# A head's Z-product records dealt unevenly over its 24 points, and one weight load moved ahead of a wait

## The reference

```python
h = rms_norm(x, g_norm[l]) * (1.0 + scale) + shift
proj = h @ w_in[l]
xa, va, oa, za, ia, fa, qa, ka, vat, zb, ga, gb = jnp.split(proj, split_at, axis=-1)
xc = jax.nn.silu(causal_depthwise_conv(xa, w_conv[l], b_conv[l]))
# q_m, k_m: xc times small matrices; 4 heads of width 256, chunked recurrence over the tokens
h_m = mlstm_chunkwise(q_m, k_m, v_m, ia + b_igate[l], fa + b_fgate[l])
h_m = rms_norm(sigmoid(oa) * h_m, g_mlstm_head[l]) + skip_mlstm[l] * xc
y_m = (h_m * jax.nn.silu(za)) @ w_out_mlstm[l]
# three attention groups (window, dilation) per head, merged by a softmax over their log-denominators
o_a = jnp.sum(wts[..., None] * jnp.stack(outs, axis=0), axis=0)
y_a = (o_a * jax.nn.silu(zb)) @ w_out_attn[l]
merged = jax.nn.sigmoid(ga) * y_m + jax.nn.sigmoid(gb) * y_a
x = x + gate * (merged @ w_out[l])
return rms_norm(x, g_final)
```

## Time and profile before

| | us |
|---|---|
| median of 3 runs (lowest, highest) | 1370.96 (1369.63, 1371.36) |
| the profiled execution: its own time | 1371.11 |
| its span in the profile | 1369.3 |
| PE busy | 1345.7 (98%) |
| DVE, ACT, POOL busy | 855.3, 580.1, 463.0 |
| chain that ended last: share of PE | 87% |

### The profile page before, as it was taken

One profiled execution on the slowest core, in us unless ns is written; L12 is line 12 of the kernel. 1 busy time (PEld: TensorE's weight loads), 2 busy tenths in 40 slices (PEclk: granted clock), 3 DMA queues, 4 the chain that ended last, 5 costly groups with the idle time before them and its releaser, 6 DMA issues.

```text
span 1369.3 us, 17469 instructions
## 1 busy us (share of the span) xinstructions
PE 1345.7 (98%) x6453; PEld 1126.9 (82%) x6453; DVE 855.3 (62%) x1472; ACT 580.1 (42%) x1016; POOL 463.0 (34%) x298
## 2 busy tenths in 40 slices
PE   8999999999999999999999999999999999999998
PEld 6888888888888888888898788889878887888886
DVE  7988766573745444535368757866875766434586
ACT  7663353343444344332545446354545534111122
POOL 0096555554545555543002200210120022222551
PEclk9999999999999999999999999999999999999999
DMA  8522323323234343337231841553172165453543
GB/s 316 196 82 95 132 99 123 123 93 115 101 123 139 123 143 134 139 112 228 73 83 48 231 93 32 161 148 94 48 227 67 33 241 205 128 187 140 173 138 108
DMA packets 65454, 180.52 MB, mean 132 GB/s; under 512 B 22001, under 2 KB 22129, under 8 KB 63318
## 3 DMA queue, kind: packets, MB, share of 16 engines
q1 hardware_dynamic: 61082, 166.64, 36.9%
q10 hardware_dynamic: 3168, 8.70, 1.9%
q0 software_dynamic: 1120, 4.06, 1.0%
HBM read 132.49 MB, written 46.89 MB: 131 GB/s over the span
## 4 chain that ended last, share of the span: by engine, by line
PE 87%; DVE 6%; ACT 3%; DMA 2%; issue 1%; SPq 0%; POOL 0%; ACTq 0%; DVEq 0%
PE banks L592 23%; PE banks L594 23%; PE banks L593 23%; PE banks L1265 4%; PE banks L1390 2%; PE banks L1400 2%; PE banks L1350 2%; PE banks L1356 2%; DMA wraw<-in_w_all 1%; PE banks L1339 1%; PE banks L1348 1%; PE banks L1409 1%; PE banks L584 1%; PE banks L556 1%; PE banks L1378 1%
## 5 line engine op out<-in xcount | busy, mean ns | idle before, releaser
L1248 POOL TENSOR_TENSOR wlo<-wraw,whi 128x1024 fp32r<-128x1024 f32 x28 | 72.1, 2575 | 436.5 <-ACT whi L1468 411.1
L718 POOL TENSOR_TENSOR wlo<-w_sum,whi 128x512 fp32r<-128x512 f32 x112 | 165.2, 1477 | 137.4 <-ACT whi L843 137.4
L592 PE MATMUL banks<-t_hi,whi 128*128 128x512 f32 x448 | 174.3, 389 | 0.0
L593 PE MATMUL banks<-t_lo,whi 128*128 128x512 f32 x448 | 174.3, 389 | 0.0
L594 PE MATMUL banks<-t_hi,wlo 128*128 128x512 f32 x448 | 174.3, 389 | 0.0
L989 DVE TENSOR_TENSOR c_sum<-c_sum,banks 128x512 f32<-128x512 f32 x196 | 134.4, 686 | 44.7 <-PE banks L594 30.6
L592 PE MATMUL banks<-h_hi,whi 128*128 128x512 f32 x416 | 162.0, 389 | 0.0
L594 PE MATMUL banks<-h_hi,wlo 128*128 128x512 f32 x416 | 161.9, 389 | 0.0
L593 PE MATMUL banks<-h_lo,whi 128*128 128x512 f32 x416 | 161.8, 389 | 0.0
L843 ACT ACTIVATE whi<-w_sum 128x512 fp32r<-128x512 f32 x112 | 70.5, 630 | 165.5 <-PE banks L594 100.7
L592 PE MATMUL banks<-whi,h_hi 128*128 128x512 f32 x256 | 100.2, 391 | 1.4 <-POOL wlo L1248 1.4
(11 more groups left out here) (374 smaller groups left out, 2904.8 us busy)
## 6 DMA issues: line engine op xcount, KB each, us to landing
wraw<-in_w_all SPq DMA_DIRECT2D x72, 512.0 KB, 4.3
raw<-in_w_all SPq DMA_DIRECT2D x28, 512.0 KB, 4.4
queries_keys<-fin SPq DMA_DIRECT2D x12, 1024.0 KB, 4.0
qa<-queries_keys SPq DMA_DIRECT2D x12, 768.0 KB, 13.7
s_wada<-in_w_ada_cols SPq DMA_DIRECT2D x16, 512.0 KB, 8.2
attn_values<-fin SPq DMA_DIRECT2D x6, 1024.0 KB, 4.0
tn<-attn_values SPq DMA_DIRECT2D x12, 512.0 KB, 10.1
sig_c<-merge_gates SPq DMA_DIRECT2D x6, 1024.0 KB, 6.4
```

The source lines that it names most:

```text
L592: t_.matmul(out, w_hi, x_hi, start=first, stop=False)
L593: t_.matmul(out, w_hi, x_lo, start=False, stop=False)
L718: nc.gpsimd.tensor_tensor(wlo4[:, o % 4, :], source(r, j), whi4[:, o % 4, :].bitcast(F32), subtract).then_inc(s_split, 1)
L1248: nc.gpsimd.tensor_tensor(to, wraw[:, q % 2, :], hi.bitcast(F32), ALU.subtract).then_inc(w_split, 1)
```

## The change

The 96 records of a head are dealt out by a table of sizes: 4, 4, 6, 7 for the points 0 to 3, 3 for the points 4 to 15, 4 for 16 to 18, then 7, 4, 4, 6, 6 for 19 to 23. A record is now found by its running number, so that a product can end inside a point. The four products end at points 4, 12, 19 and 23 (`formed_at`). ACT's `keep` stands ahead of `mixing(u)` at 4, 12 and 23, and behind `mixing(19)` for the third; the `next_high` that went with the second is now at point 12.

In SP's program the next head's load of its chunk n = 3 (the fourth token chunk, and its fifth load) is issued behind the load of `ct`, ahead of the wait for `cw_done`.

```diff
-    PARTS_OF, RECORDS = 6, 4
-    POINTS = 2 * PARTS_OF * (MAIN - ZA)
+    RECORDS = 3 * KT
+    SIZES = (4, 4, 6, 7) + 12 * (3,) + 3 * (4,) + (7, 4, 4, 6, 6)
+    ENDS = list(itertools.accumulate(SIZES))
+    POINTS = len(SIZES)
...
+    def formed_at(n, h):
+        return next(u for u in range(POINTS) if ENDS[u] >= (2 * (n - ZA) + h + 1) * RECORDS)
... SP
             sp.dma_start(ct[:].rearrange("p g c w -> p g (c w)"), stat_d.rearrange("g (p c) w -> p g (c w)", c=NCH)).then_inc(ct_in, 16)
+            if i + 1 < HEADS:
+                load(HEAD0 + (i + 1) * CHUNKS + AHEAD)
             sp.wait_ge(cw_done, i + 1)
...
-                load(HEAD0 + i * CHUNKS + p + AHEAD)
+                if p or not i:
+                    load(HEAD0 + i * CHUNKS + p + AHEAD)
... PE
+            for u in range(POINTS):
+                for record in range(ENDS[u] - SIZES[u], ENDS[u]):
+                    project(record)
+                if u == 1:
+                    head_q()
...
+                mixing(u)
... ACT
+            for u in range(POINTS):
+                if u == formed_at(ZA, 0):
+                    keep(ZA, 0)
+                if u == formed_at(ZA, 1):
+                    keep(ZA, 1)
+                    next_high(ZA + 2)
+                if u == formed_at(ZA + 1, 1):
+                    keep(ZA + 1, 1)
+                    next_high(ZA + 3)
...
+                mixing(u)
+                if u == formed_at(ZA + 1, 0):
+                    keep(ZA + 1, 0)
```

More of the change, by code:

```diff
@@ L1 @@
+import itertools
 from contextlib import ExitStack
@@ L1122, in mix @@
     STATS = (1, 4, 2)
-    PARTS_OF, RECORDS = 6, 4
-    POINTS = 2 * PARTS_OF * (MAIN - ZA)
+    RECORDS = 3 * KT
+    SIZES = (4, 4, 6, 7) + 12 * (3,) + 3 * (4,) + (7, 4, 4, 6, 6)
+    ENDS = list(itertools.accumulate(SIZES))
+    POINTS = len(SIZES)
     SCORES, ATTEND, NORM, TURN = 3, 3, 19, 23
-    def point(n, h, part):
-        return 2 * PARTS_OF * (n - ZA) + PARTS_OF * h + part
+    def formed_at(n, h):
+        return next(u for u in range(POINTS) if ENDS[u] >= (2 * (n - ZA) + h + 1) * RECORDS)
     def mlstm_step(u):
@@ L1256, in tensor, with project @@
         for i in range(0, HEADS):
-            def project(n, h, part):
+            def project(record):
+                (n, h), e = divmod(record // RECORDS, 2), record % RECORDS
+                n += ZA
                 to = ring_slot(i, n)
-                if part == 0:
+                if e == 0:
                     pe.wait_ge(w_split, chunk(i, n) + 3)
                     pe.wait_ge(kept[1 if n == ZA else h], i * MAIN + n + 1)
[L1262 to L1267, removed]
+                k, third = divmod(e, 3)
+                w, x = ((whi, h_hi), (whi, h_lo), (wlo, h_hi))[third]
+                mm = t_.matmul(ps[:, h, :], w[:, to, k * P:(k + 1) * P], x[:, k, h * HALF:(h + 1) * HALF],
+                               start=(e == 0), stop=(e == RECORDS - 1))
+                if e == RECORDS - 1:
                     mm.then_inc(proj, 1)
@@ L1429, in tensor @@
             fold_weights()
[L1430 to L1439, removed]
+            for u in range(POINTS):
[3 more added lines that the diff above has]
+                    head_q()
+                if (i, u) == (0, 2):
+                    pe.wait_ge(decays_in, 32)
+                    t_.transpose(M1[:, 0:P], gr[:], ident[:]).then_inc(hc_turned, 1)
+                mixing(u)
     def scalar(act):
@@ L1602, in scalar @@
             next_high(5)
[L1603 to L1622, removed]
+            for u in range(POINTS):
[7 more added lines that the diff above has]
+                    next_high(ZA + 3)
+                if u == 1:
+                    exp_table()
+                    for j in range(4):
+                        head_keep(j)
+                if u == 2:
+                    if i == 0:
+                        head_decays()
+                    intra_weights()
+                mixing(u)
+                if u == formed_at(ZA + 1, 0):
+                    keep(ZA + 1, 0)
+                if u == TURN - 2:
+                    z_sigmoid(ZA)
+                    z_sigmoid(ZB)
             z_sigmoid(ZA + 1)
```

## The result

| | before | after |
|---|---|---|
| median (lowest, highest), us | 1371.16 (1369.63, 1371.76) | 1379.36 (1378.21, 1380.28) |
| runs beside each other | 4 | 4 |
| profiled execution: own time | 1371.11 | 1378.53 |
| its span | 1369.3 | 1376.7 |
| PE busy | 1345.7 (98%) | 1351.8 (98%) |

The ratio is 1.0061, with an interval of 1.0044 to 1.0078. The changed kernel is slower by 8.2 us where 3.4 less had been forecast. PE's share still reads 98%, although its busy time has grown by 6 us on the same matmuls.

A forecast was written before the change was run, and what follows sets the result against it. PE, busy 98% of the span, was taken as the bound. Tail 6.1 plus load 1.7 minus middle 4.4 gave 3.4 us less: 1367.6 for a median of runs, with an 8-in-10 range of 1363.2 to 1370.6.

The forecast's parts named there:

- The load ahead: Passages between heads: the earlier SP load removes PE's wait for `wlo` at two passages, 1.7 us less in all.
- The tail: Points 19 to 23: seven more records remove three PE waits at point 20 and the `og` turn, 1.52 us per head.
- Point 4 and the other short points: Points 4 to 15 except 13: PE stands 0.2 us per head at point 4 and nowhere else.
- Point 13: Values product: later `hin` delays DVE's `pT`, so PE stands 0.9 us per head, bounds 0 and 1.4.
- What the short middle adds, per head: Points 4 to 15, one record less each: 0.2 plus 0.9 us per head, 4.4 us in all, between 0 and 6.5.
- the rule of the shared ports: Passage between heads: DVE with two SBUF inputs and POOL exclude each other; sum the same or 0.1 to 0.3 us worse.
- Slower: Points 4 on: the chain between engines bounds, all 12 records return as standing; 3.2 us slower, 1374.2; rival's chance 0.08.

The follow-up runs named there:

- the copies moved behind point 12: Changed kernel with ACT's second Z copy and the next chunk's rounding behind `mixing(12)` instead of ahead of it; 1365.03 us, ratio 0.9952 to the kernel before.
- POOL held: Changed kernel with POOL's split of the chunk rounded at point 12 waiting until DVE has copied `pT`; 1367.89 us, ratio 0.998 to the kernel before.

## Why the prediction was wrong

**The load ahead: right.** SP issues the load at 746.58 after, against 757.14 in the earlier trace rows; ACT rounds it at 763.48 and POOL begins at 764.60, and PE waits for `wlo` nowhere in the heads. The forecast had 761.1 for the rounding, by the clock of before. Head 0 is longer now, and ACT's sigmoid ahead of it starts at 762.51 and not at 760.15; behind the sigmoid the rounding starts 0.97 later, where 0.95 had been forecast.

**The tail: right.** PE after, at the values of point 20 and at the turn of `og`, against the earlier trace rows:

```profile
730.36 0.39 PE L1273 MATMUL banks<-h_lo,whi 128*128 128x512 f32 x1
730.59 0.65 PE L1408 MATMUL banks<-pT,vt 128*128 128x128 f32 x4
...
734.50 0.39 PE L1273 MATMUL banks<-h_hi,wlo 128*128 128x512 f32 x1
734.73 2.04 PE L1374 MATMUL banks<-ident,og 128*128 128x128 f32 x16
```

There is no idle time at either, and the turn comes in one piece of 2.04 in place of 2.23. The margins are 0.18 (ACT's copy ends at 730.41) and about 0.25, in the forecast's 0.1 to 0.3. All three waits went. The term was even a little low: 1.7 to 1.8 a head, as the copies moved behind point 12 show, and not 1.52.

**Point 4 and the other short points: right.** From the start of point 4's scores to its turn it is 1.07 after (673.75 to 674.82) and 0.86 before (673.28 to 674.14): 0.2. Elsewhere PE does not stand. Its margin behind DVE's copy fell by 0.23 at the values products of points 7 and 11, from 0.81 to 0.58 and from 0.47 to 0.23.

**Point 13: the step that failed.** In "What the short middle adds, per head", the term for point 13 was mis-sized: 0.9 a head, with an upper bound of 1.4, against 2.06. ACT's part was right, `hin` 0.64 later against the clock of point 10, and by itself it costs the forecast 0.9 (POOL held: 0.86). The failure is in the words that DVE "works through in one piece". That took DVE's instructions at their old lengths. The prediction moved ACT's rounding and did not follow who waits for it: POOL's split starts on that very rounding, and came with it onto DVE's chain, for 1.19 more. It weighed the rule of the shared ports for the passage between heads, where it costs nothing, and not here. There it also read its rows too mildly, as something held up "for 1.35 and not for POOL's whole 2.39". POOL's instruction of the earlier trace rows ends at 765.96 + 2.39 = 768.35, and the DVE one of the earlier trace rows that starts at 766.86 beside it ends at 766.86 + 2.57 = 769.43, 1.08 later, where it lasts 1.22 alone. DVE was held to the end of POOL's instruction, as at point 13. The bound of 1.4 was built from ACT's and PE's parts alone, and so did not hold.

**The clock: a step that was missing.** Each of the four waits brought 3.4 us at half clock in the profiled execution, 6.6 us in all. Nothing in the trace of before pointed to it in the heads: there PE never stood for more than 1.2 us at a time.

The sum with the measured terms starts from the kernel with the copies behind point 12, which has the load, the tail and the short points, but neither the wait nor the fall. Its span is 1361.2, and 1361.2 + 4 x 2.06 + 6.6 = 1376.0. The measured span is 1376.7, and the 0.7 is the 0.2 of other things in each head.

**The rivals.** "Slower" was given 0.09, and its rival 0.08, by a mechanism that is not the one that came: all twelve missing records standing, at every short point. Its threshold, 1.95 us of standing a head, was passed (2.06 + 0.2), yet nearly all of it at one point and by POOL. That a rival named the right direction is luck: its 3.2 us slower came from another place.

## What to carry to other kernels

When an instruction is moved, follow everything that it releases, on the mostly idle engines too, and ask what of the critical chain lies beside the whole length of what they then do. Behind each stall of PE, look at the granted clock and at the distance of equal matmuls before adding up: here 6.6 us of the 15 lost at point 13 were in no list of waits. Take filler only where the chain has slack, and leave the copies that others wait for where they are: the same idea with another table of sizes, and the load ahead, was worth 11 us.

## What the runs showed that I had not expected

- A DVE instruction on 128x1 with all its inputs in SBUF was held to the end of POOL's 128x1024 one: 1.41 to 1.43 us in place of 0.22, in every head of two kernels. Its neighbours were not held beside the same split: `hnb` with one input in PSUM kept 0.43, and the one-input instruction 0.15.
- Half clock for 3.4 us behind a stand of 2.06 to 2.07: four times of four in the kernel after, three of four, one of four and none of four in other kernels with the same stand, and none of four behind stands of 1.46, 0.86 and 0.33. These counts are from one profiled execution of each kernel.
- A like stretch at half clock from 28 or 29 us on in the setup of six of the profiled executions, worth up to 2.0 us, over code that is the same in all, and behind a stand of only 0.5 us and a row of one-column products. One profiled execution of each kernel is not enough to compare times that differ by less.
